# Sixteen key rows as dense blocks instead of twenty in the expert stage of a hybrid decoder layer, V products by one tile at a time, and two buffers that join late

## What is computed

```python
def peer(h, w_q, sub_keys, u, v):
    q = (hf @ w_q).reshape(T, PEER_HEADS, 2, PEER_KEY_DIM // 2)
    sc = jnp.einsum('thpc,pkc->thpk', q, sub_keys).astype(jnp.float32)
    v1, i1 = lax.top_k(sc, PEER_TOPK)
    ...
    cidx = (i1[:, :, 0, :, None] * PEER_N_KEYS + i1[:, :, 1, None, :]).reshape(T, PEER_HEADS, PEER_TOPK * PEER_TOPK)
    top, pos = lax.top_k(cand, PEER_TOPK)
    experts = jnp.take_along_axis(cidx, pos, axis=-1).reshape(T, PEER_HEADS * PEER_TOPK)
    gates = jax.nn.softmax(top, axis=-1).reshape(T, PEER_HEADS * PEER_TOPK)
    ...
        a = jax.nn.gelu(jnp.einsum('cd,ced->ce', xc, u[ec]).astype(jnp.float32), approximate=False)
        return jnp.einsum('ce,ced->cd', gc * a, v[ec].astype(jnp.float32))
```

## Time and profile before

| | |
|---|---|
| median of 3 runs | 941.77 us (939.80 to 943.84) |
| profiled execution | 945.5 us |
| its span | 943.7 us |
| granted PE clock, mean | 0.946 |
| PE busy | 849.5 us (90%) |
| DVE busy | 643.8 us (68%) |
| ACT busy | 417.9 us (44%) |
| POOL busy | 389.9 us (41%) |
| read from HBM | 343.80 MB |
| chain that ended last | PE 46%, DMA 29%, DVE 12%, ACT 7% |

### The profile page before, as it was taken

The page is one execution under the profiler, slowest core; times in us unless marked ns, Lnnn a source line. Parts: engine busy times, 40 slices in busy tenths (PEclk is TensorE's granted clock), DMA queues, the critical chain, the costliest instruction groups (busy, mean ns, idle before and its releaser), DMA issues.

```text
span 943.7 us, 15713 instructions
## 1 busy us (share of the span) xinstructions
PE 849.5 (90%) x5808; PEld 547.2 (58%) x5808; DVE 643.8 (68%) x1450; ACT 417.9 (44%) x1069; POOL 389.9 (41%) x307
## 2 busy tenths in 40 slices
PE   9999999999998768778779999879989979897997
PEld 8998998799977534344336666535545423232332
DVE  5433676465566987889898778899878554444565
ACT  5534555444574565445554444443333322222252
POOL 1000055131003487366564433555657664453461
PEclk9999999999999999798889999978989789899999
DMA  8897534256435999999999999989999999999994
GB/s 306 239 196 206 182 124 144 87 226 228 149 137 191 341 406 416 369 416 417 417 410 396 411 361 398 375 331 400 398 370 402 415 410 414 407 387 408 373 390 197
DMA packets 55028, 303.20 MB, mean 321 GB/s; under 512 B 11515, under 2 KB 14959, under 8 KB 21777
## 3 DMA queue, kind: packets, MB, share of 16 engines
q0 software_dynamic: 37152, 225.29, 59.8%
q1 hardware_dynamic: 14968, 74.03, 21.8%
q10 hardware_dynamic: 2832, 2.88, 2.2%
HBM read 343.80 MB, written 1.54 MB: 366 GB/s over the span
## 4 chain that ended last, share of the span: by engine, by line
PE 46%; DMA 29%; DVE 12%; ACT 7%; issue 5%; POOL 2%; POOLq 0%; SPq 0%; DVEq 0%; ACTq 0%
DMA arena<-in_experts,arena 19%; PE y L1192 13%; PE ps L1231 7%; DMA raw<-in_panels 6%; PE ps L806 4%; PE ps L807 4%; PE ps L808 4%; DVE late_ring L2199 3%; DVE w_lo L1766 3%; PE y L1264 3%; ACT w_hi L1346 2%; PE ps L1251 2%; DMA late_ring<-in_experts,expert 2%; PE ps L849 2%; DMA late_ring<-in_experts,arena 1%
## 5 line engine op out<-in xcount | busy, mean ns | idle before, releaser
L2199 DVE CUSTOM_DVE_ANT_0 late_ring<-arena 128x1024 f32<-128x1024 f32 x172 | 209.2, 1223 | 106.6 <-DMA arena<-in_experts,arena 104.0
L2408 POOL DMA_INDIRECT arena<-in_experts,arena x160 | 214.3, 1340 | 161.8 <-PE ps L1195 124.6
L1195 PE MATMUL ps<-arena,diag 64*64 64x512 f32 x784 | 214.9, 674 | 0.0
L1192 PE MATMUL y<-arena,diag 64*64 64x512 f32 x520 | 146.1, 686 | 39.1 <-ACT diag L1580 39.0
L1192 PE MATMUL y<-late_ring,diag 64*64 64x512 f32 x432 | 117.2, 666 | 35.1 <-ACT diag L1580 34.5
L1566 ACT ACTIVATE acts<-dots 128x2 f32<-128x2 f32 x124 | 25.2, 203 | 264.8 <-DVE dots L2199 263.3
L1766 DVE TENSOR_TENSOR w_lo<-raw,w_hi 128x2048 fp32r<-128x2048 f32 x36 | 84.9, 2361 | 74.2 <-ACT w_hi L1346 74.2
L2408 POOL DMA_INDIRECT late_ring<-in_experts,arena x62 | 81.6, 1316 | 98.4 <-PE ps L1195 85.0
L2199 DVE CUSTOM_DVE_ANT_0 late_ring<-late_ring,arena 128x1024 f32<-128x1024 f32 x79 | 96.0, 1219 | 36.4 <-DMA late_ring<-in_experts,arena 32.1
L1192 PEld LDWEIGHTS y<-arena,diag 64*64 64x64 f32 x520 | 34.5, 147 | 119.1 <-ACT diag L1580 63.9
L1346 ACT CAST w_hi<-raw 128x2048 fp32r<-128x2048 f32 x37 | 70.5, 1904 | 58.0 <-DMA raw<-in_panels 40.8
(11 more groups left out here) (344 smaller groups left out, 1741.0 us busy)
## 6 DMA issues: line engine op xcount, KB each, us to landing
raw<-in_panels SPq DMA_DIRECT2D x40, 1024.0 KB, 4.9
arena<-in_panels SPq DMA_DIRECT2D x6, 1024.0 KB, 6.8
x<-in_up SPq DMA_DIRECT2D x10, 512.0 KB
late_ring<-in_up SPq DMA_DIRECT2D x10, 512.0 KB
x<-in_experts SPq DMA_DIRECT2D x10, 512.0 KB
late_ring<-in_experts SPq DMA_DIRECT2D x10, 512.0 KB
arena<-line_scratch ACTq DMA_DIRECT2D x8, 320.0 KB, 8.9
arena<-in_experts,arena POOLq DMA_INDIRECT x160
```

The costliest lines, as they stand in the source:

```text
L1192: straight = pe.matmul(y[rows, t, cols], diag[rows, a % DIAGS, rows], slot(a)[rows, down], start=False, stop=False, skip_group_check=True)
L1195: across = pe.matmul(ps[to, half, :], diag[rows, b % DIAGS, rows], slot(b)[rows, down], start=first, stop=False, skip_group_check=True)
L2199: i = nc.vector.tensor_tensor_reduce(row if n < len(FIRST_BUFFERS) else products[s % GROUP], row, h_rows[:, u // PEER_HEADS, :], 1.0, 0.0, ...
L2408: nc.gpsimd.indirect_dma_start(out=slot(n), out_offset=None, in_=experts, in_offset=bass.IndirectOffsetOnAxis(ap=expert_rows(u)[:, s:s + 1 ...
```

## The change

Sixteen key rows are blocks instead of 20: four more are gathered. The U products stand behind groups 36 to 51. Units are routed from earlier slots (7, then 6 apart, where it was 8). The one-hot steps start at slots 112 to 172, every 4. The V products go by block and tile, 32 halves evenly behind groups 92 to 114. Buffer 11 comes back at slot 190, behind the last `token_gates`, and a new buffer 16, over `rowsT`, joins at slot 196, behind the last `weigh_acts`. The last unit's slots 0 to 9 go by `use_pair`, the sum of the crossed products comes behind them, and six slots stay single. The final squares of tile 0 stand behind group 117, its scaling behind slot 238.

```diff
-BUFFERS = 16
-SINGLES_FROM = 8
+BUFFERS = 17
+SINGLES_FROM = 10
...
-BLOCKS = 20
+BLOCKS = 16
...
-LATE_ROUTES = {8: 20, 3: 29, 4: 40, 9: 48, 5: 56, 10: 64, 6: 72, 7: 80, 11: 88, 12: 96, 13: 104, 14: 112, 15: 120}
+LATE_ROUTES = {8: 20, 3: 29, 4: 42, 9: 50, 5: 57, 10: 64, 6: 71, 7: 78, 11: 85, 12: 91, 13: 97, 14: 103, 15: 109}
...
-UP_FROM = 37
+UP_FROM = 36
...
-LISTS_BEHIND = {47: 0, 66: 1}
-LISTS_AT = {98: 0, 136: 1}
+LISTS_BEHIND = {46: 0, 61: 1}
+LISTS_AT = {97: 0, 127: 1}
...
-    begun = 110 + 6 * q if q < 4 else 132 + 4 * (q - 4)
+    begun = 112 + 4 * q
...
+DOWN_FROM, DOWN_TO = 92, 115
 DOWN_BEHIND = {}
 for b in range(BLOCKS):
-    DOWN_BEHIND.setdefault(94 + b * 26 // BLOCKS, []).append(b)
+    for t in range(TILES):
+        group = DOWN_FROM + (TILES * b + t) * (DOWN_TO - DOWN_FROM) // (TILES * BLOCKS)
+        DOWN_BEHIND.setdefault(group, []).append((b, t))
+FINISHED_BEHIND, FINISHED_AT = 117, 238
...
-JOINS = {22: 14, 24: 15, 58: 6, 67: 7, 79: 1}
-GIVEN_FROM = {15: 67, 14: 71, 10: 87, 11: 97, 12: 101}
+JOINS = {22: 14, 24: 15, 58: 6, 67: 7, 79: 1, 190: 11, 196: 16}
+JOINED_BEHIND = {190: "token_gates15"}
+GIVEN_FROM = {15: 67, 14: 70, 10: 85, 11: 97, 12: 100}
+BACK = {JOINS[n]: n for n in (190, 196)}
...
-            def weigh_block(block):
+            def weigh_block(block, t):
...
-                for t in range(TILES):
-                    for half in range(2):
-                        cols = slice(half * 512, (half + 1) * 512)
-                        mm = pe.matmul(y[:, t, cols], in_block_acts[:, block, t * P:(t + 1) * P], down[:, cols],
-                                       start=False, stop=False, skip_group_check=True)
-                mm.then_inc(blocks_weighed if block == BLOCKS - 1 else table_used, 1)
+                for half in range(2):
+                    cols = slice(half * 512, (half + 1) * 512)
+                    mm = pe.matmul(y[:, t, cols], in_block_acts[:, block, t * P:(t + 1) * P], down[:, cols],
+                                   start=False, stop=False, skip_group_check=True)
+                if t:
+                    mm.then_inc(blocks_weighed if block == BLOCKS - 1 else table_used, 1)
...
             for g in range(SINGLES_FROM // GROUP):
-                use_group(1, last_unit + g)
-                if g == 1:
-                    sum_crossed(1)
+                use_pair(1, last_unit + g, False)
+            sum_crossed(1)
...
+                if i == FINISHED_BEHIND:
+                    act.wait_ge(blocks_weighed, 1)
+                    final_squares(0)
 
             for g in range(SINGLES_FROM // GROUP):
                 weigh(UNITS - 1, g)
-                if g == 0:
-                    take_crossed(1)
-                if g == 1:
-                    act.wait_ge(blocks_weighed, 1)
-                    final_squares(0)
+            take_crossed(1)
...
+                if n == FINISHED_AT:
+                    dve.wait_ge(final_row_in, 16)
+                    finish(0)
+
             for s in range(TOPK):
                 dot((UNITS - 1) * TOPK + s)
-                if s == 5:
-                    finish(0)
```

More of the change, by code:

```diff
@@ L168, in ring_order @@
     for n in range(SLOTS):
-        waiting = [b for b in waiting if GIVEN_FROM.get(b, SLOTS) > n]
+        waiting = [b for b in waiting if not GIVEN_FROM.get(b, SLOTS) <= n < BACK.get(b, SLOTS)]
         b = JOINS[n] if n in JOINS else waiting.pop(0)
@@ L178 @@
 BUFFER_OF_SLOT, SLOT_BEFORE = ring_order()
-LAST_IN = {b: max(n for n, other in enumerate(BUFFER_OF_SLOT) if other == b) for b in GIVEN_FROM}
+LAST_IN = {b: max(n for n, other in enumerate(BUFFER_OF_SLOT[:BACK.get(b, SLOTS)]) if other == b) for b in GIVEN_FROM}
 PLACE_OF = {"ocross1": OWN_PLACE, "qpeer0": PANELS.index("qcross0") % SPLIT_RING,
@@ L496, in at_buffer @@
         def at_buffer(b):
+            if b == BUFFERS - 1:
+                return rowsT[:].rearrange("p k c -> p (k c)")
             return ring[:, b, :] if b < RING else late_ring[:, LATE[b - RING], :]
@@ L1301, in _ @@
                     token_gates(GATHER_GATES_BEHIND[i])
-                for block in DOWN_BEHIND.get(i, ()):
-                    weigh_block(block)
+                for block, tile in DOWN_BEHIND.get(i, ()):
+                    weigh_block(block, tile)
                 if i == first_of_tile + 1 and t:
@@ L1676, in take_up, with final_squares @@
                                           ACT.Gelu))
+            def final_squares(t):
+                nc.scalar.activation(x[:, t, :], y[:, t, :], ACT.Square,
+                                     accum_out=sumsq[:, NORM["final"], t:t + 1]).then_inc(sumsq_ready, 1)
+                act.wait_ge(meansq_ready, NORM["final"] + t + 1)
+                nc.scalar.activation(root[:, NORM["final"], t:t + 1], meansq[:, NORM["final"], t:t + 1],
+                                     ACT.Sqrt).then_inc(root_ready, 1)
             for i in range((UNITS - 1) * TOPK // GROUP):
@@ L2309, in list_last_rows, with finish @@
                                       last_rows_f[:].rearrange("p a b -> p (a b)")).then_inc(last_rows_ready, 1)
+            def finish(t):
+                n = NORM["final"]
+                dve.wait_ge(sumsq_ready, TILES * n + t + 1)
+                nc.vector.tensor_scalar(meansq[:, n, t:t + 1], sumsq[:, n, t:t + 1], 1.0 / D, EPS, ALU.mult, ALU.add
+                                        ).then_inc(meansq_ready, 1)
+                dve.wait_ge(root_ready, n + t + 1)
+                nc.vector.reciprocal(rstd[:, n, t:t + 1], root[:, n, t:t + 1]).then_inc(rstd_ready, 1)
+                dve.wait_ge(rstd_ready, n + t + 1)
+                for half in range(2):
+                    cols = slice(half * 512, (half + 1) * 512)
+                    nc.vector.scalar_tensor_tensor(x[:, t, cols], y[:, t, cols], rstd[:, n, t:t + 1],
+                                                   g_final_row[:, cols], ALU.mult, ALU.mult
+                                                   ).then_inc(final_ready, 1)
             for n in range((UNITS - 1) * TOPK):
@@ L2329, in _ @@
                     list_last_rows()
-            def finish(t):
-                n = NORM["final"]
-                dve.wait_ge(sumsq_ready, TILES * n + t + 1)
-                nc.vector.tensor_scalar(meansq[:, n, t:t + 1], sumsq[:, n, t:t + 1], 1.0 / D, EPS, ALU.mult, ALU.add
-                                        ).then_inc(meansq_ready, 1)
-                dve.wait_ge(root_ready, n + t + 1)
-                nc.vector.reciprocal(rstd[:, n, t:t + 1], root[:, n, t:t + 1]).then_inc(rstd_ready, 1)
-                dve.wait_ge(rstd_ready, n + t + 1)
-                for half in range(2):
-                    cols = slice(half * 512, (half + 1) * 512)
-                    nc.vector.scalar_tensor_tensor(x[:, t, cols], y[:, t, cols], rstd[:, n, t:t + 1],
-                                                   g_final_row[:, cols], ALU.mult, ALU.mult
-                                                   ).then_inc(final_ready, 1)
-            dve.wait_ge(final_row_in, 16)
+                if n == FINISHED_AT:
+                    dve.wait_ge(final_row_in, 16)
+                    finish(0)
             for s in range(TOPK):
                 dot((UNITS - 1) * TOPK + s)
-                if s == 5:
-                    finish(0)
                 if s >= SINGLES_FROM:
@@ L2429, in _ @@
                     pool.wait_ge(product_ready, PLACE["qpeer1_1"] + 1)
-                if n in JOINS:
+                if n in BACK.values():
+                    if n in JOINED_BEHIND:
+                        pool.wait_ge(product_ready, PLACE[JOINED_BEHIND[n]] + 1)
+                    else:
+                        pool.wait_ge(blocks_gated, TOKEN_CHUNKS // 2)
+                elif n in JOINS:
                     over = [name for name in LOADED_EARLY if LOADED_EARLY[name] == JOINS[n]]
```

8 lines of the change are left out of this document (1 added, 7 removed).

## The result

The changed kernel takes 946.60 us (median of 9 runs, 944.81 to 950.91); the kernel before, beside it, 940.66 (9 runs, 938.72 to 943.84). The ratio is 1.0061, with a 95% interval of 1.0040 to 1.0082: 5.7 us or 0.6% slower. The forecast of 943.6 lay 3 us too low, and the time falls just past the bound of 0.5% into what I had given 0.29. The profiled execution took 947.84 us, its span is 946.0.

The account below looks back on a forecast made before the run. DMA was taken to bound the kernel, with losses below 415 GB/s where PE or DVE is full. The terms 10.5 - 2.1 - 1.5 - 6.6 + 1.5 made +1.8 us, so 943.6 us, range 929 to 954.

Parts of the forecast that it names:

- what I had given 0.29: Whole kernel: the chance given to the change being slower by over 0.5%.
- What bounds it: Whole kernel: DMA share 0.93 to 1.00 in all but the end; byte count the floor, distance from 415 GB/s the loss.
- Bytes, +10.5: Slots 0 to 252: 8.39 MB more gathered, 4.19 MB of tables fewer, priced by stretch rates: +10.5 us.
- the 29.7 us of PE work that I booked at 0: U and V products: eight fewer blocks save PE 29.7 us, hidden as before: 0, bounds 0 and -6.1 us.
- Late buffers and halved V blocks, -6.6: Slots 192 to 252: two more buffers and half blocks lift 395 to 412 GB/s: -6.6 us, bounds 0 and -7.7.
- The last unit, +1.5: Kernel's end: five pairs, then the crossed sum between slots 249 and 250, then six singles: +1.5 us, bounds 0 and +3.
- The squares moved, 0: Final squares of tile 0 moved to group 117: twelve buffers cover ScalarE's 2.2 us wait for DVE, so 0.
- DVE work that moves, -2.1 and -1.5: Routing moved earlier: still fits slots 72 to 119 (0); -2.1 us in slots 120 to 135, -1.5 in 136 to 191.
- Never dry: Faster rival: slots 72 to 191 run at 412 GB/s too, giving 934 us; chance 0.33.
- DVE binds: Slower rival: denser DVE work stretches slots 72 to 119 to 139 to 140 us, giving 952 us; chance 0.15.
- The late buffers bring nothing, as the clock falls: Slower rival, slots 192 to 239: PE gaps lower the clock, the 6.6 us do not come, 950 us; chance 0.12.

Follow-up runs that it names:

- a_finish_back: The changed kernel with only the final squares and the scaling of tile 0 back in the last unit: 947.34 us, ratio 1.0070 to the kernel before.

## Why the prediction was off, point by point

The 5.7 us fall into three parts. Routing, halves and late buffers together are worth -1.7 (20 blocks, old end); put in one by one they gave +0.2, -0.8 and -1.3, none of them clear of zero, which makes -1.9. Four blocks fewer cost +3.9 with the old end, and +4.6 with the new one. The new end costs +3.6 with 16 blocks, and +2.8 with 20 (1.0012 against 0.9982, plus or minus 2.5). Each part was thus measured twice, over different neighbours, and the two values agree within far less than their intervals, which are near 3 us: the order of sizes is shown, the last microsecond is not. That the forecast lay only 3 to 4 us off is partly luck. The bytes were booked some 6 us too dear, and that hid most of what the other terms had wrong the other way: late buffers and halves were to give 4.5 us more than they gave, DVE's moved work was to give 3.6 and alone gave nothing in the kernel before, and the end cost 1 to 2 more.

- **What bounds it: right, but its measure was not.** DMA stands at 0.97 to 1.01 in all stretches up to slot 239. The byte count is not the floor, though, since skipped rows take time on the queue too. That slots 0 to 71 gave +5.8 for +5.9 is luck: 4.0 MB more moved there (163.05 us at 397 GB/s, 168.83 at 407), not the 2.4 of an even share, and each at little more than half the price that I gave it.
- **Bytes, +10.5: this step failed in its price.** The MB came as counted, but I priced each at the average rate of its stretch, as if a skipped row took no time. The queues' own time grew by 4.7 us, and the measured price of four blocks fewer is 3.9 to 4.6. Whether the 29.7 us of PE work that I booked at 0 gave anything besides is not shown; in slots 72 to 119, where I had put its bound of -6.1, nothing came (133.74 us, with 20 blocks 132.45).
- **Late buffers and halved V blocks, -6.6: this step failed.** One by one they bring 0.8 and 1.3 us with 20 blocks, and over slots 192 to 252 the rate stayed at 394 GB/s. The 412 came in slots 192 to 239 only, and without the late buffers they were still 409. I had read POOL's 58.5 us of waiting as what two buffers take away. It is the wait of an issuer whose ring is full, and with two more buffers it was 61.9. The rest of the higher rate goes with the number of blocks, so this term booked what belongs to the one above.
- **The last unit, +1.5: right in direction, too small.** It measured 3.6 and 2.8, the first just above its bound of 3. From the end of dot 249 (922.56) I had 6.2 us up to the end of the sum, and it took 7.8. Weights and diagonals took 1.5 for 1.4, copy and sum 1.01 and 1.93 as booked. The pair took 3.2 us, not 1.9, at the lower level of the clock. Further, I had counted only PE. That ACT stands before the copy, and DVE behind ACT for 3.82 us, keeps slots 250 and 251 back while their bytes are there. PE was then full from slot 250 on, as forecast. That the clock falls with the pairs is seen in slots 240 to 252: it is 0.77 by pairs with PE busy for 23.13 of 32.89 us, and 0.94 by whole diagonals with 26.93 of 30.66; in all profiles it is 0.77 to 0.84 with pairs and 0.94 to 1.00 with whole diagonals. How much of the cost is the clock's is not shown: with the squares put back the last pair took 1.9 us at the full level, and the median was no lower. I had warned of the clock for slots 192 to 239, where it stayed at 0.95, and not for the slots where pairs took the place of groups. The Trainium skill, TensorE: Matmul & The Clock Gate, section HAM oscillation, says that gaps between bursts of work bring the lower level back; the trace agrees, with 3.04 us of idle time ahead of a pair that went from 0.66 to 1.07 us per matmul; a gap of 2.71 us in `a_finish_back` did not bring it back.
- **The squares moved, 0: not contradicted.** Putting them back gave +0.8, plus or minus 3.1.
- **DVE work that moves, -2.1 and -1.5: right in place.** Slots 72 to 119 hold 118.45 us of DVE, where I had 117, in 133.74 us, where I had 131.6; DVE did not bind there (the stretch was to be 139 to 140), though its hole of 276 GB/s moved in. Slots 120 to 135 gained 3.4 us, more than booked. But what the move is worth depends on the rest: 5.3 us in the change, nothing in the kernel before, where DVE has the same room in that stretch (30.59 of 36.74 us) and the stretch keeps its length. There it is the four blocks that make the difference; by what, no run shows.
- **The rivals.** "Never dry" fell: slots 72 to 119 ran at 385 GB/s, 136 to 191 at 403. "DVE binds" fell. "The late buffers bring nothing, as the clock falls" is half right: they bring about 1 us, but the clock did not fall there and 412 GB/s came all the same.

Left open: whether PE's lighter work has any part in the 412 GB/s of slots 192 to 239, and why single pieces of 10 us, such as the earlier trace rows at 379 with a share of 0.98, have a full share and a low rate.

## What to carry to other kernels

The wait of an issuer for a free buffer says that the ring is full, and not what a longer ring would bring; that is to be read from the consumer's waits for landings and from what keeps it busy. When a step is moved close to the end of a kernel, follow what is queued behind it on every engine that takes part: a copy that waits for TensorE can hold ScalarE, and by it VectorE, for work whose data have landed. A row that a gather skips is not free: where a change turns skipped rows into fetched ones, price it by the time of the queue's packets, not by bytes at an average rate. And when a stretch gets a better rate while several things change, one run with each part alone tells which of them it belongs to.
